# First half of a mixing block's merged tile: turned by DMA transposes instead of TensorE

## What is computed

```python
for l in range(DEPTH):                       # 2 mixing blocks
    h = rms_norm(x, norm_g[l])
    p = h @ w_in[l]                          # all projections
    y_a = short_conv_mixer(...) ; y_b = sparse_attention_mixer(...) ; y_c = pool_mixer(...)
    g = sigmoid(mgate).reshape(B, S, 3, D)
    merged = g[:, :, 0] * y_a + g[:, :, 1] * y_b + g[:, :, 2] * y_c
    x = x + merged @ w_o[l]
```

## Time and profile before

| | |
|---|---|
| median of 3 runs | 1538.21 us (1538.20 to 1538.69) |
| the profiled execution | 1537.75 us |
| its span, first to last instruction | 1536.0 us |
| granted TensorE clock, mean | 1.000 |
| HBM read | 278.24 MB |

### The profile page before, as it was taken

One profiled execution on the slowest core, in us unless ns is written; L12 is line 12 of the kernel. 1 busy time (PEld: TensorE's weight loads), 2 busy tenths in 40 slices (PEclk: granted clock), 3 DMA queues, 4 the chain that ended last, 5 costly groups with the idle time before them and its releaser, 6 DMA issues.

```text
span 1536.0 us, 18866 instructions
## 1 busy us (share of the span) xinstructions
PE 1526.1 (99%) x7155; PEld 1258.8 (82%) x7155; DVE 996.7 (65%) x1220; ACT 810.3 (53%) x1028; POOL 368.8 (24%) x392
## 2 busy tenths in 40 slices
PE   9999999999999999999999999999999999999999
PEld 7888888788888888877878888887888888788887
DVE  5666567566555656466676665568966666896664
ACT  5554455565444544456766444466365446637542
POOL 2333020013420344011101342023541101354110
PEclk9999999999999999999999999999999999999999
DMA  9865763277567674665536755664645457464553
GB/s 311 248 214 166 267 210 125 84 219 243 172 204 242 194 238 140 214 216 178 179 129 220 222 188 192 213 244 149 216 142 179 171 193 253 154 217 138 178 177 125
DMA packets 261575, 298.12 MB, mean 194 GB/s; under 512 B 80469, under 2 KB 174853, under 8 KB 261504
## 3 DMA queue, kind: packets, MB, share of 16 engines
q1 hardware_dynamic: 258880, 289.11, 57.5%
q0 software_dynamic: 2480, 8.03, 1.6%
q10 hardware_dynamic: 144, 0.03, 0.0%
HBM read 278.24 MB, written 1.07 MB: 182 GB/s over the span
## 4 chain that ended last, share of the span: by engine, by line
PE 91%; DVE 4%; ACT 3%; issue 1%; POOL 1%; DMA 0%; ACTq 0%; DVEq 0%; POOLq 0%
PE ACC L943 25%; PE ACC L950 24%; PE ACC L944 24%; PE ZB L1108 2%; PE ACC L871 1%; PE ACC L1138 1%; PE ACC L1140 1%; PE ACC L1139 1%; DVE WL L2568 1%; PE TB L968 1%; DVE YC L2580 1%; PE ACC L1243 1%; PE ACC L1027 1%; PE ACC L1028 1%; PE ACC L1245 1%
## 5 line engine op out<-in xcount | busy, mean ns | idle before, releaser
L2267 DVE TENSOR_TENSOR WL<-RAW,WH 128x2048 fp32r<-128x2048 f32 (+2 forms) x256 | 520.3, 2072 | 198.6 <-ACT WH L1516 197.7
L1516 ACT ACTIVATE WH<-RAW 128x2048 fp32r<-128x2048 f32 (+3 forms) x254 | 419.4, 1699 | 155.5 <-PE ACC L950 97.3
L943 PE MATMUL ACC<-WH,XH 128*128 128x512 f32 (+2 forms) x1272 | 491.2, 387 | 0.3 <-DVE XL L2296 0.2
L944 PE MATMUL ACC<-WH,XL 128*128 128x512 f32 (+2 forms) x1272 | 488.1, 385 | 0.0
L950 PE MATMUL ACC<-WL,XH 128*128 128x512 f32 (+2 forms) x1272 | 334.4, 385 | 0.2 <-DVE WL L2267 0.2
L943 PEld LDWEIGHTS ACC<-WH,XH 128*128 128x128 f32 x1272 | 238.9, 188 | 50.8 <-issue 2.0
L944 PEld LDWEIGHTS ACC<-WH,XL 128*128 128x128 f32 x1272 | 239.0, 188 | 46.3
L950 PEld LDWEIGHTS ACC<-WL,XH 128*128 128x128 f32 x1272 | 236.2, 188 | 48.1 <-DVE WL L2267 0.6
L2112 POOL COPY HID<-TURNED 128x512 uint16<-128x512 uint16 x88 | 113.4, 1331 | 169.7 <-DMA TURNED<-PLANES 169.7
L1620 ACT ACTIVATE SIDE<-ACC,RX 128x256 f32<-128x256 f32 x88 | 41.1, 473 | 203.0 <-PE ACC L950 202.9
L943 PE MATMUL ACC<-WH,HH 128*128 128x512 f32 x352 | 137.3, 390 | 0.0
(11 more groups left out here) (331 smaller groups left out, 1952.7 us busy)
## 6 DMA issues: line engine op xcount, KB each, us to landing
RAW<-w_in_in SPq DMA_DIRECT2D x66, 1024.0 KB, 6.4
RAW<-ffn_w_gate_in SPq DMA_DIRECT2D x42, 1024.0 KB, 5.1
RAW<-ffn_w_up_in SPq DMA_DIRECT2D x42, 1024.0 KB, 7.5
RAW<-ffn_w_down_in SPq DMA_DIRECT2D x32, 512.0 KB, 4.5
RAW<-ffn_w_down_in SPq DMA_DIRECT2D x16, 1024.0 KB, 6.9
RAW<-mlstm_w_in_in SPq DMA_DIRECT2D x16, 1024.0 KB, 7.3
RAW<-ffn_w_down_in SPq DMA_DIRECT2D x16, 768.0 KB, 6.1
RAW<-attn_w_in_in SPq DMA_DIRECT2D x12, 1024.0 KB, 7.2
```

Of the source, the lines that this page charges most:

```text
L943: nc.tensor.matmul(bank, lh, wh[:, i, :], start=first and i == 0, stop=False)
L944: nc.tensor.matmul(bank, ll, wh[:, i, :], start=False, stop=False)
L1516: nc.scalar.activation(WH[:, slot, lo:hi], RAW[:, slot, lo:hi], ACT.Copy).then_inc(hi_ready, 1)
L2267: nc.vector.tensor_tensor(WL[:, slot, lo:hi], RAW[:, slot, lo:hi], WH[:, slot, lo:hi].bitcast(F32), ALU.subtract).then_inc(lo_ready, 1)
```

## The change

The first half of the merged tile becomes a seventh DMA turn, "merged". POOL makes its planes (in KT2, whose contents are used up by then) once block 21 is evacuated, SP issues the two transposes ahead of the load of block 25's weights, and POOL merges the turned planes into YT. ACT's task rounds YT into XH and DVE's task subtracts into XL, each half behind the other; both sit in slot 46 instead of 45. TensorE's task is empty, and TensorE waits for DVE's subtractions (`merged_lo`) ahead of the output product. The second half of the tile is turned on TensorE as before.

```diff
-        MIX_TURNS = ("q", "k", "conv_in", "conv_gate", "pool_gate", "attn_out")
+        MIX_TURNS = ("q", "k", "conv_in", "conv_gate", "pool_gate", "attn_out", "merged")
...
+                          merged=turn_buffer("PMG", both(sbuf_at["KT2"])))
...
+                          merged=turn_buffer("TMG", both(sbuf_at["KT2"] + 2 * HALF_TILE)))
...
-        MIX_MERGED = dict(q=QM, k=KT2[:, 0], conv_in=CM, conv_gate=CM, pool_gate=YT, attn_out=YT)
+        MIX_MERGED = dict(q=QM, k=KT2[:, 0], conv_in=CM, conv_gate=CM, pool_gate=YT, attn_out=YT, merged=YT)
...
-        task(45, "merged")
+        task(46, "merged")
...
-        MIX_TURN_BEFORE = {8: "q", 10: "k", 11: "conv_in", 13: "conv_gate", 15: "pool_gate", 20: "attn_out"}
+        MIX_TURN_BEFORE = {8: "q", 10: "k", 11: "conv_in", 13: "conv_gate", 15: "pool_gate", 20: "attn_out", 25: "merged"}
...
-                             norms=lambda kind: None, rotate=lambda kind: None, merged=lambda: merged(0))
+                             norms=lambda kind: None, rotate=lambda kind: None, merged=lambda: None)
...
-                at.rounded += KD // 2
+                at.rounded += KD // 4
+                pe.wait_ge(merged_lo, 2 * (layer + 1))
                 out_product(lambda: merged(1))
...
+                def merged():
+                    act.wait_ge(weights_used, at.chunk)
+                    for g in range(2):
+                        act.wait_ge(hidden_merged, mix_turn(layer, "merged", g))
+                        nc.scalar.activation(XH[:, 2 * g:2 * g + 2, :], YT[:, 2 * g:2 * g + 2, :], ACT.Copy).then_inc(merged_hi, 1)
...
-                tasks.update(norms=lambda kind: None, rotate=lambda kind: None, merged=lambda: activations((0, 1)))
+                tasks.update(norms=lambda kind: None, rotate=lambda kind: None, merged=merged)
...
-                    elif name == "attn_out":
-                        pool.wait_ge(branch_ready, 3 * layer + 2)
+                    elif name in ("attn_out", "merged"):
+                        pool.wait_ge(branch_ready, 3 * layer + (2 if name == "attn_out" else 3))
...
                 turn("attn_out", AG[:, :, :])
+                pool.wait_ge(blocks_used, at.block + 23)
+                turn("merged", mid[0])
...
+                def merged():
+                    for g in range(2):
+                        dve.wait_ge(merged_hi, 2 * layer + g + 1)
+                        part = slice(2 * g, 2 * g + 2)
+                        nc.vector.tensor_tensor(XL[:, part, :], YT[:, part, :], XH[:, part, :].bitcast(F32), ALU.subtract).then_inc(merged_lo, 1)
...
-                             norms=norms, rotate=lambda kind: rotate(kind) if kind in ("q", "k") else None, merged=lambda: activations((0, 1)))
+                             norms=norms, rotate=lambda kind: rotate(kind) if kind in ("q", "k") else None, merged=merged)
```

More of the change, by code:

```diff
@@ L309, in both @@
             return at, at + HALF_TILE
-        MIX_TURNS = ("q", "k", "conv_in", "conv_gate", "pool_gate", "attn_out")
+        MIX_TURNS = ("q", "k", "conv_in", "conv_gate", "pool_gate", "attn_out", "merged")
         MIX_PLANES = dict(q=turn_buffer("PQ", both(sbuf_at["YT"])), k=turn_buffer("PK", both(sbuf_at["YT"])),
                           conv_in=turn_buffer("PCI", both(units_at)), conv_gate=turn_buffer("PCG", both(sbuf_at["ST"])),
-                          pool_gate=turn_buffer("PPG", both(sbuf_at["SX"])), attn_out=turn_buffer("PAO", both(units_at)))
+                          pool_gate=turn_buffer("PPG", both(sbuf_at["SX"])), attn_out=turn_buffer("PAO", both(units_at)),
+                          merged=turn_buffer("PMG", both(sbuf_at["KT2"])))
         MIX_TURNED = dict(q=turn_buffer("TQ", both(sbuf_at["SX"])), k=turn_buffer("TK", both(sbuf_at["ST"])),
@@ L317, in program @@
                           pool_gate=turn_buffer("TPG", (spare_at, units_at + 2 * HALF_TILE)),
-                          attn_out=turn_buffer("TAO", both(units_at + 2 * HALF_TILE)))
+                          attn_out=turn_buffer("TAO", both(units_at + 2 * HALF_TILE)),
+                          merged=turn_buffer("TMG", both(sbuf_at["KT2"] + 2 * HALF_TILE)))
         QM = KT2[:, 0]
         CM = sb("CM", [P, 4, SEQ], offset=sbuf_at["BH"])
-        MIX_MERGED = dict(q=QM, k=KT2[:, 0], conv_in=CM, conv_gate=CM, pool_gate=YT, attn_out=YT)
+        MIX_MERGED = dict(q=QM, k=KT2[:, 0], conv_in=CM, conv_gate=CM, pool_gate=YT, attn_out=YT, merged=YT)
         def small(name, shape):
@@ L428, in program @@
         second_turned = sem("second_turned")
+        merged_hi = sem("merged_hi")
+        merged_lo = sem("merged_lo")
         gains_folded = sem("gains_folded")
```

## The result

The changed kernel took 1545.4 us (median of 5 runs, 1544.77 to 1546.26) against 1538.2 us for the kernel before (median of 5, 1536.34 to 1538.69). It is slower: the medians differ by 7.2 us, a quotient of 1.0047; the ratio on record, 1.0054 with a 95% interval of 1.0044 to 1.0065, is a little higher and would be 8.3 us. The profiled execution has a span of 1543.2 us against 1536.0, and a mean granted clock of 0.998 where it was 1.000.

The account below looks back on a forecast made before the run. TensorE, busy for 99% of the span, was taken to bound the kernel. The profiled 1537.75 us plus 2 x 2.96 us lost gave 1543.7 us, with a range of 1541.9 to 1547.6.

Parts of the forecast that it names:

- Removed: Between blocks 22 and 23, TensorE loses eight transposes per mixing block, so the output product could begin 0.87 us earlier.
- Turn: After block 21: planes by 1233.1, transposes landing 3.6 to 3.9 us after issue, POOL's merges from 1235.9 to 1238.7.
- The new wait: Ahead of the output product, TensorE waits for DVE's subtractions behind 4.50 us of low parts: 2.20 us lost per block.
- POOL meets the low parts: POOL's last merge copy runs against DVE's low parts, adding 0.76 us: 2.96 us lost per block; the forecast, chance 0.52.
- the rival in which POOL stays clear: Transposes land 2.7 us after issue, merges end at 1237.5 before the low parts: 2.20 us per block, 1542.15; chance 0.20.
- The clock: Behind the new stall TensorE's clock falls from 2.4 to 1.2 GHz, slowing the first output half: 1549.1 us; chance 0.10.
- Covered edits: SP's later second output load, DVE's later evacuation of block 23 and POOL's otherwise idle time were costed at nothing.

Follow-up runs that it names:

- no_turn: The kernel before without any turn of the merged tile's first half (no transposes, rounding or subtraction): 1535.53 us against 1537.5, ratio 0.9989.
- fill: The changed kernel with 14 more matmuls, result unused, on TensorE ahead of its wait for the subtractions: 1541.68 us, ratio 1.0028 to the kernel before.
- moved_only: The kernel before, TensorE's transposes kept, with only ACT's rounding and DVE's subtraction of the first half moved to slot 46: 1542.63 us, ratio 1.0041.

## Why the prediction was right, point by point

The direction, the range and the mechanism of the new wait held; the size was 7.2 us where 5.9 was forecast, and 3.5 us of the loss came from the clock, which I had left out of the forecast.

- *Removed.* 0.87 us per block, by the chain: no_turn, which leaves out the roundings and subtractions too, shows 2.0 us for both, with an interval that holds 1.74.
- *Turn.* Forecast for the first block: planes 4.4 us (1228.68 to 1233.1), measured 4.21; merges from 3.9 us after the first issue, measured 1234.12 - 1230.81 = 3.3. The transposes landed in 2.9 to 3.2 us in the first block and 3.8 to 4.2 in the second; I had taken 3.6 to 3.9 for both.
- *The new wait.* Low parts, then subtraction, then TensorE, as written. 2.20 was the price with POOL clear of the low parts; the first block, where POOL's merges ended at 1236.95 and the low parts began at 1237.00, measured 2.14.
- *POOL meets the low parts.* True in the second block only. DVE's pair took 5.04 us, 0.54 more than alone, and not 0.76; 2.68 lost where I had 2.96. So the first block followed the rival in which POOL stays clear (0.20), the second the forecast, and 2.96 for both was too high by 0.82 and 0.28.
- *The clock.* This is the step that failed. I gave its fall 0.10 and wrote that the stall is short and that nothing in the trace shows a fall; it fell in both blocks of the profiled execution, from 2.4 to 1.2 GHz by the spacing of 0.43 instead of 0.23 us, and fill shows that it does not fall when TensorE has work during the stall. My price of 2.7 us per block, half of the first output half, was too high: 1.73 and 1.75 were measured. The Trainium skill's rule (TensorE: Matmul & The Clock Gate, Part 1), that the clock falls back when TensorE idles and returns after sustained work, agrees with these runs in its direction: the spacing is 0.43 us behind the stall and 0.23 again from 1247.36 on. These runs do not show which stall will do it: one of moved_only's two stalls of 2.0 us was followed by a fall, the other was not.
- *What the trace of before did show of it.* I read the earlier trace rows as a wait of 1.7 us with the clock at 1.00. That wait is TensorE's wait for its first work in the run, and slow matmuls stand directly behind it. In the chain of the kernel before (two lines, then the clock by stretch) eight matmuls take 3.78 us at the start and eight of the same line 2.06 us a little later, although the clock column has 1.00 there. So matmuls about twice as slow stood in that trace, and whether the clock made them so is not shown. What it had no example of is a stall of 2 us or more in the middle of the work, where the longest wait was 1.1 us; the chance of a fall could not be read from it.

```profile
1.72 3.78 PE ZB L1495 x8
...
7.29 2.06 PE ZB L1495 x8
...
0.00:4.00 4.00, 2.28 (x5) 1.82 (x6) 0.70 (x1) 1.23 (x1) 0.50 (x7) 1.00 0.51 121
```

- *Covered edits.* The later second load and the later evacuation cost nothing: at full clock the first output half takes 5.44 us (fill) and no wait of TensorE but the one for XL appeared.

The errors worked against each other: 2 x 2.96 = 5.9 us forecast, 4.8 for the stalls and 3.5 for the clock measured, less the 1.1 us by which the executions differ beforehand. That 1545.4 us lies within 1541.9 to 1547.6 is thus in part luck: I had left the clock case out of that range, and it came true.

## What to carry to other kernels

When a transfer takes over an engine's work, place its consumers by what their streams hold ahead of them and not by when the data come: here the data waited 4.5 us behind ACT's high parts and DVE's low parts, and the same change with its rounding and subtraction put first cost nothing that could be measured. Price the removed instructions by their share of the chain (0.87 us for eight), not by their durations (2.2 us), before paying for them. And count a new stall of TensorE with the slow matmuls behind it: stalls of 2.0 to 3.4 us cost about 1.7 us more each when the clock fell.

## What the runs showed of the hardware that was not expected

The granted clock fell behind stalls of 2.9 and 3.4 us, and behind one of two stalls of 2.0 us in the same execution, so a stall's length alone did not decide it. What else did is not shown. Transposes of an identity held the clock at 1.00 as matmuls did. With POOL's plane copies beside them, DVE's short low parts took 2.77 us instead of 2.35; in moved_only, which has no such copies, they took 2.35. And the clock column reads 1.00 at the start of the run, where eight matmuls took 3.78 us that took 2.06 us a little later.
